# The query norm of the first layer's dense heads as one number per query, in the scale of the softmax's exponential

## The chip, the cores and the metric

The kernel runs on one core of a Trainium2 chip. The metric is the device time of one execution in microseconds (us). Five engines work side by side, each through its own queue in a fixed order: TensorE (PE; its loads of the stationary operand are shown as PEld), VectorE (DVE), ScalarE (ACT), GpSimd (POOL) and SyncE (SP), which here issues the large transfers. They meet by semaphores only.

## The reference

The program is an attention layer, a pooling layer and a second attention layer with a retention half, over 512 tokens of width 2048. The change touches the eight dense heads of the first layer. For these the reference computes, with 512 queries, 512 + 256 keys and a head size of 128:

```python
qA = _rope(_rmsnorm(qA, q_norm), cos, sin)
kA = _rope(_rmsnorm(kA, k_norm), cos, sin)
outA = _dense_attention(qA, jnp.concatenate([kA, kA_c], axis=1), jnp.concatenate([vA, vA_c], axis=1))

def _rmsnorm(x, g):
    y = xf * lax.rsqrt(jnp.mean(xf * xf, axis=-1, keepdims=True) + EPS)
    return (y * g.astype(jnp.float32)).astype(x.dtype)

# dense attention, per block of 128 queries
s = jnp.einsum('bqkgd,bskd->bkgqs', qb, k) * ATTN_SCALE
p = jax.nn.softmax(s, axis=-1)
```

The norm of a query is one number, so it can be left out of the rotation and of the product with the keys, and multiplied in afterwards: softmax(r s) needs exp(r s - max(r s)), and with r > 0 the maximum is r max(s).

## The kernel before

**Layout.** Queries and keys lie transposed: the 128 dimensions of a head on the partitions, the 512 tokens along the free axis. `QR[:, h % 2, :]` holds one head's queries, `KTA` the keys of four key heads, `VV` the values. The score of 128 queries against 768 keys lies in the PSUM tile `S` (queries on the partitions), of which there is one. The dense heads are 0 to 7; heads 8 to 15 are banded, without a norm. `TB` and `OB` are single PSUM banks for sums, transposes and the output of a head; `G` are four banks in two pairs, in which the projections are summed up.

**The stream that TensorE works through.** A projection unit makes 256 columns of `w_in` in four chunks of 512 rows. Each weight chunk is loaded to `RAW` by SP, rounded to `WHI` by ScalarE, its rest taken to `WLO` by VectorE (L1314), three buffers each; it is used in four steps of six matmuls (`G<-HHI,WHI`, `G<-HLO,WHI`, `G<-HHI,WLO` twice). A pair of heads, `p`, has two units: one for the gates z and one for the queries, so 32 steps in all. When the queries of pair p are done, `q_copy` takes the two banks to `QR`, and the task `pair_task(p)` then runs beside the 32 steps of the next pair: after each step one yield of the generator passes, and what it puts into the plan at that point stands there in the queue of every engine. The plan thus sets the order on all engines; nothing is moved at run time.

**pair_task before, dense pairs.** For each of the two heads in turn, `norm_rope` puts: the square (`nr_square`, ScalarE, `SQ2[1]`), two steps later the sum over the partitions (`nr_stat`: TensorE multiplies a matrix of ones with the squares, 128x512, into `TB`; ScalarE takes logarithm and exponential of all 128x512 into `TY`; VectorE makes `TM<-TB` and refines the root with three more instructions over 128x512), and a step later `nr_apply` (VectorE: query times gain times root into `TM`, L1320, then the rotation, four instructions at L1314). That is 8 steps, one more follows, and then the eight scores of the pair stand three steps apart: `score` (TensorE, `S<-KTA,QR`), `softmax` (VectorE: negated maximum of the row, L1501; ScalarE: `PB<-S,SM`, exp(S + nm), with the sum, L1132; VectorE: reciprocal L1510, product L1317), four or five steps later `turn` (transposes of `PB` into `TB` and `OB`, copied to `PT` by ScalarE), and seven steps after the fourth score of a head `pv` (`OB<-PT,VV`) and `gate`. Since there is one `S`, the matmuls of a score wait for the exponential of the score before (`a_exp`). In VectorE's queue the reciprocal stands right behind the maximum, so VectorE waits for each exponential.

**What else is in the same queues.** After every chunk one load of 512 KB for the modulation of later layers is multiplied up by VectorE (`mod_acc`, four instructions `MACC`, L1320); for every fourth of these `mod_sum` transposes the sums in `TB` (TensorE) and reduces them (VectorE, L1437). It is put in at a chunk's end or, if one is pending, right behind the next score. The gates' `silu_a` and `silu_b` follow behind the first unit of a pair.

## Time and profile before

| | |
|---|---|
| time, median of 3 runs | 2726.67 us (2721.63 to 2731.41) |
| profiled execution, its own time | 2726.54 us |
| its span | 2724.8 us |
| granted TensorE clock over the span | 0.975 of full |
| TensorE busy | 2596.8 us, 95% of the span |
| VectorE busy | 1728.5 us, 63% |
| ScalarE busy | 949.7 us, 35% |
| chain that ended last, by engine | PE 76%, DVE 14%, DMA 3%, ACT 3%, issue 3% |

The numbers come from one profiled execution. Busy time is a sum over stages that have different limits, so a stage is read by stretches. The dense heads of the first layer lie between 280 and 600 us of the span (the pairs start at about 280, 354, 432 and 508 us), the banded ones behind them up to 866 us. A wait is the idle time of an engine in front of an instruction, put down to what released it; the clock is a share of full speed, 2.4 GHz.

### The profile page before, as it was taken

The numbers are of one execution on the slowest core, as the hardware profiler recorded it, in microseconds if no ns is written. First come the engines' busy times: TensorE is split into PE (matmuls) and PEld (weight loads), VectorE is DVE, ScalarE is ACT, GpSimd is POOL, SyncE is SP. The second block draws the span as 40 slices with busy tenths as digits, with TensorE's granted clock in tenths as the row PEclk, the third lists the DMA queues.
The fourth block names the chain that finished last, engine by engine and source line by source line (L and its number), as shares of the span: only waits on it lengthen the run. The fifth ranks groups of instructions, "written<-read, shape, count | busy, mean of one in ns | idle before, by whom it ended". The sixth has DMA issues, their size and how long they took to land.

```text
span 2724.8 us, 31894 instructions
## 1 busy us (share of the span) xinstructions
PE 2596.8 (95%) x12675; PEld 2084.8 (77%) x12675; DVE 1728.5 (63%) x2880; ACT 949.7 (35%) x1510; POOL 134.2 (5%) x121
## 2 busy tenths in 40 slices
PE   7999999999988999999998998999999999999898
PEld 4789666677766887888776886877878878878686
DVE  4446777767775877777887877667465444445422
ACT  3232343343343333332323333344354422223221
POOL 0000000000000103000010112000000000000000
PEclk7999999999999998999999997999999999999999
DMA  9935433333334553656647553444222222322432
GB/s 349 328 134 161 132 99 105 118 113 124 122 107 147 197 185 128 205 169 205 190 155 244 188 182 134 141 142 147 70 78 86 82 82 89 98 83 82 150 117 70
DMA packets 358566, 390.71 MB, mean 143 GB/s; under 512 B 11842, under 2 KB 352450, under 8 KB 354578
## 3 DMA queue, kind: packets, MB, share of 16 engines
q1 hardware_dynamic: 352144, 354.79, 40.8%
q0 software_dynamic: 6128, 33.89, 3.3%
q8 instruction: 100, 1.64, 0.3%
q14 instruction: 48, 0.39, 0.0%
q10 hardware_dynamic: 146, 0.00, 0.0%
HBM read 371.85 MB, written 16.78 MB: 143 GB/s over the span
## 4 chain that ended last, share of the span: by engine, by line
PE 76%; DVE 14%; DMA 3%; ACT 3%; issue 3%; SPq 1%; POOL 0%; DVEq 0%; ACTq 0%; POOLq 0%
PE G L1765 63%; PE S L1765 5%; PE OB L1765 5%; DVE MACC L1320 4%; PE TB L1765 2%; DVE WLO L1314 2%; PE TB L1768 1%; DMA MRAW<-in_od_mod_w 1%; DMA MRAW<-in_w_ada 1%; DVE TT L1314 1%; ACT WHI L1006 1%; DMA MRAW<-in_ev_mod_w 1%; DVE Y L1314 1%; DVE SM L1501 1%; ACT PB L1132 1%
## 5 line engine op out<-in xcount | busy, mean ns | idle before, releaser
L1765 PE MATMUL G<-HHI,WHI 128*128 128x512 f32 x2624 | 1109.8, 423 | 41.0 <-issue 18.2
L1765 PE MATMUL G<-HHI,WLO 128*128 128x512 f32 x2624 | 1034.1, 394 | 0.0
L1765 PE MATMUL G<-HLO,WHI 128*128 128x512 f32 x2624 | 1031.6, 393 | 0.0
L1765 PEld LDWEIGHTS G<-HHI,WHI 128*128 128x128 f32 x2624 | 499.2, 190 | 165.5 <-issue 50.2
L1314 DVE TENSOR_TENSOR WLO<-RAW,WHI 128x1024 fp32r<-128x1024 f32 x376 | 458.2, 1221 | 259.8 <-ACT WHI L1006 257.0
L1006 ACT ACTIVATE WHI<-RAW 128x1024 fp32r<-128x1024 f32 x376 | 395.0, 1053 | 580.3 <-PE G L1765 539.7
L1765 PEld LDWEIGHTS G<-HLO,WHI 128*128 128x128 f32 x2624 | 499.4, 190 | 114.7 <-issue 19.2
L1765 PEld LDWEIGHTS G<-HHI,WLO 128*128 128x128 f32 x2624 | 497.2, 189 | 109.4
L1320 DVE SCALAR_TENSOR_TENSOR MACC<-MRAW,SC,MACC 128x256 f32<-128x256 f32 x840 | 431.8, 514 | 94.7 <-DMA MRAW<-in_od_mod_w 36.3
L1765 PE MATMUL G<-WHI,HHI 128*128 128x256 f32 x640 | 186.8, 292 | 0.0
L1765 PE MATMUL G<-WLO,HHI 128*128 128x256 f32 x640 | 181.5, 284 | 0.0
L1765 PE MATMUL G<-WHI,HLO 128*128 128x256 f32 x640 | 181.5, 284 | 0.0
L1132 ACT ACTIVATE PB<-S,SM 128x768 f32<-128x768 f32 (+2 forms) x64 | 52.6, 822 | 281.4 <-DVE SM L1317 161.1
L1765 PEld LDWEIGHTS G<-WHI,HHI 128*128 128x128 f32 x640 | 123.0, 192 | 8.0 <-issue 7.4
L1003 ACT ACTIVATE SQ<-SQ 128x512 f32<-128x512 f32 x144 | 90.8, 631 | 100.3 <-DVE SQ L1320 97.3
L1765 PEld LDWEIGHTS G<-WHI,HLO 128*128 128x128 f32 x640 | 123.1, 192 | 2.3 <-issue 1.7
L1765 PEld LDWEIGHTS G<-WLO,HHI 128*128 128x128 f32 x640 | 123.1, 192 | 0.0
L1765 PE MATMUL S<-KTA,QR 128*128 128x256 f32 (+2 forms) x256 | 86.0, 459 | 19.0 <-ACT PB L1132 19.0
L1765 PEld LDWEIGHTS S<-KTA,QR 128*128 128x128 f32 x256 | 47.3, 192 | 49.1 <-ACT PB L1132 24.6
L1765 PE MATMUL OB<-PT,VV 128*128 128x512 f32 (+2 forms) x192 | 77.0, 552 | 0.7 <-ACT PT L1006 0.7
L1317 DVE TENSOR_SCALAR TM<-TB 128x512 f32<-128x512 f32 (+1 forms) x36 | 24.3, 675 | 83.8 <-ACT TY L1003 83.8
L1003 ACT ACTIVATE TY<-TB,SM 128x512 f32<-128x512 f32 (+1 forms) x36 | 24.4, 678 | 141.0 <-PE TB L1765 141.0
(263 smaller groups left out, 2399.1 us busy)
## 6 DMA issues: line engine op xcount, KB each, us to landing
RAW<-in_w_in SPq DMA_DIRECT2D x128, 512.0 KB, 3.9
MRAW<-in_od_mod_w SPq DMA_DIRECT2D x96, 512.0 KB, 4.9
MRAW<-in_w_ada SPq DMA_DIRECT2D x96, 512.0 KB, 5.1
RAW<-in_ev_w_in SPq DMA_DIRECT2D x80, 512.0 KB, 3.9
RAW<-in_od_w_in SPq DMA_DIRECT2D x64, 512.0 KB, 4.1
MRAW<-in_ev_mod_w SPq DMA_DIRECT2D x54, 512.0 KB, 5.1
RAW<-in_ev_w_out SPq DMA_DIRECT2D x32, 512.0 KB, 3.5
RAW<-in_od_w_out SPq DMA_DIRECT2D x32, 512.0 KB, 3.5
```

Of the source, the lines that this page charges most:

```text
L1003: return e.o.activation(o, i, fn, bias=bias, scale=scale)
L1006: return e.o.activation(o, i, ACT.Copy, scale=scale)
L1132: e.o.activation(PB[n % 2][:, lo:768], S[:, lo:768], ACT.Exp, bias=nm, scale=1.0, accum_out=SM[:, i + 1:i + 2]).then_inc(*a_exp.up((h, qt)))
L1314: return e.o.tensor_tensor(o, a, b, op)
L1317: return e.o.tensor_scalar(o, a, s1, s2, op0, op1) if op1 else e.o.tensor_scalar(o, a, s1, None, op0)
L1320: return e.o.scalar_tensor_tensor(out=o, in0=a, scalar=s, in1=b, op0=op0, op1=op1)
L1501: e.o.tensor_reduce(nm, S[:, lo:768], AX_X, MAX, negate=True).then_inc(*v_sm.up((h, qt, "row"), (h, qt, "max")))
L1765: return e.o.matmul(o, l, r, start=start, stop=stop, skip_group_check=True)
L1768: return e.o.transpose(o, i, IDN[:, :])
```

## The change

The query copy of a dense head now multiplies by the gain (which already holds the factor 128^-0.5) on its way from `G` to `QR`, and ScalarE squares straight from `G` (into `SQ2[1]` and `TM`). The rotation runs on these, without the root. The sums of squares of both heads of a pair are made at once, as eight matmuls with the squares as the stationary operand and one column of ones as the moving one, so that they come out as a column of 128 queries each: `TB[:, 0:8]`. Mean, logarithm, exponential and refinement are made on 128x8. The root of a query then stands on the same partition as its score: the exponential takes it as its scale, and the negated maximum is multiplied by it in one more VectorE instruction. The generator yields five times ahead of the first score, where it did nine times.

```diff
+    QMEAN, QTEMP, QROOT = COL[:, 0:8], COL[:, 8:16], COL[:, 16:24]
+    QSQ = [SQ2[1], TM]
...
         def pair_task(p):
-            for i in range(2):
-                for _ in norm_rope(("q", 2 * p + i), p < 4):
-                    yield
+            yield
+            put("nr_apply", ("q", 2 * p))
+            yield
+            if p < 4:
+                put("q_stat", p)
+            yield
+            put("nr_apply", ("q", 2 * p + 1))
+            yield
+            if p < 4:
+                put("q_root", p)
             yield
...
+    def q_root_of(h, qt):
+        return QROOT[:, h % 2 * 4 + qt:h % 2 * 4 + qt + 1]
...
-                cp(QR[:, nt, :], G[pair][nt][:, :], SCALE if p >= 4 else 1.0).then_inc(*a_ev.up(("q", h)))
+                if p >= 4:
+                    cp(QR[:, nt, :], G[pair][nt][:, :], SCALE).then_inc(*a_ev.up(("q", h)))
+                else:
+                    e.wait_ge(v_intro, "q_scale")
+                    cp(QR[:, nt, :], G[pair][nt][:, :], COL[:, 152:153]).then_inc(*a_ev.up(("q", h)))
+                    e.wait_ge(*chain)
+                    if p:
+                        e.wait_ge(p_stat, ("q", p - 1))
+                    elif nt == 0:
+                        e.wait_ge(*sq[1])
+                    af(QSQ[nt][:, :], G[pair][nt][:, :], ACT.Square).then_inc(*a_sq.up(("q", h)))
+                    sq[1] = p_stat, ("q", p)
+            elif stage == "q_stat":
+                p, = a
+                e.wait_ge(v_rs, (("q", p), 1))
+                af(QROOT, QMEAN, ACT.Ln).then_inc(*a_rs.up((("q", p), 1)))
+                e.wait_ge(a_rs, (("q", p), 1))
+                af(QROOT, QROOT, ACT.Exp, 0.0, -0.5).then_inc(*a_rs.up((("q", p), 2)))
...
-                e.o.activation(PB[n % 2][:, lo:768], S[:, lo:768], ACT.Exp, bias=nm, scale=1.0,
+                e.o.activation(PB[n % 2][:, lo:768], S[:, lo:768], ACT.Exp, bias=nm,
+                               scale=1.0 if banded(h) else q_root_of(h, qt),
                                accum_out=SM[:, i + 1:i + 2]).then_inc(*a_exp.up((h, qt)))
...
-                if what == "kc" or what == "k" and h < 2 or what == "q" and h < 8:
+                if what == "kc" or what == "k" and h < 2:
...
+            elif stage == "q_stat":
+                p, = a
+                e.wait_ge(p_stat, ("q", p))
+                ts(QMEAN, TB[:, 0:8], 1.0 / 128, EPS, MUL, ADD).then_inc(*v_rs.up((("q", p), 1)))
+                sq[1] = p_stat, ("q", p)
+            elif stage == "q_root":
+                p, = a
+                e.wait_ge(a_rs, (("q", p), 2))
+                tt(QTEMP, QROOT, QROOT, MUL).then_inc(*v_rs.up((("q", p), 2)))
+                e.wait_ge(v_rs, (("q", p), 2))
+                stt(QTEMP, QTEMP, -0.5, QMEAN, MUL, MUL).then_inc(*v_rs.up((("q", p), 3)))
+                e.wait_ge(v_rs, (("q", p), 3))
+                stt(QROOT, QTEMP, 1.5, QROOT, ADD, MUL).then_inc(*v_rs.up((("q", p), 4)))
...
-                    *v_sm.up((h, qt, "row"), (h, qt, "max")))
-                if banded(h):
-                    e.wait_ge(v_sm, (h, qt, "row"))
+                    *v_sm.up((h, qt, "row")))
+                e.wait_ge(v_sm, (h, qt, "row"))
+                if not banded(h):
+                    e.wait_ge(v_rs, (("q", h // 2), 4))
+                    ts(nm, nm, q_root_of(h, qt), None, MUL).then_inc(*v_sm.up((h, qt, "max")))
+                else:
...
-                gf[pair][nt] = a_ev, ("q", 2 * p + nt)
+                gf[pair][nt] = (a_ev if p >= 4 else a_sq), ("q", 2 * p + nt)
+            elif stage == "q_stat":
+                p, = a
+                e.wait_ge(*tb)
+                for nt in range(2):
+                    e.wait_ge(a_sq, ("q", 2 * p + nt))
+                    for n in range(4):
+                        t = mm(TB[:, 4 * nt + n:4 * nt + n + 1], QSQ[nt][:, n * P:(n + 1) * P], ONE[:, 0:1], True, True)
+                t.then_inc(*p_stat.up(("q", p)))
+                tb = v_rs, (("q", p), 1)
```

The order on VectorE, from the second head of pair 0 to its first softmax. Before:

```order
L1317 TENSOR_SCALAR TM<-TB 128x512
L1314 TENSOR_TENSOR TT<-TY 128x512
L1320 SCALAR_TENSOR_TENSOR TT<-TT,TM 128x512
L1320 SCALAR_TENSOR_TENSOR TY<-TT,TY 128x512
L1320 SCALAR_TENSOR_TENSOR TM<-QR,COL,TY 128x512
L1314 TENSOR_TENSOR TT<-TM,SN 64x512 x2
L1314 TENSOR_TENSOR QR<-TM,CS 128x512
L1314 TENSOR_TENSOR QR<-QR,TT 128x512
L1314 TENSOR_TENSOR WLO_71<-RAW_65,WHI_68 128x1024
L1317 TENSOR_SCALAR MACC_76<-MRAW_74,SC 128x256
L1320 SCALAR_TENSOR_TENSOR MACC_76<-MRAW_74,SC,MACC_76 128x256 x3
L1501 TENSOR_REDUCE SM<-S 128x1
```

The same stretch after the change:

```order
L1347 TENSOR_SCALAR COL<-TB 128x8
L1344 TENSOR_TENSOR TT<-QR,SN 64x512 x2
L1344 TENSOR_TENSOR QR<-QR,CS 128x512
L1344 TENSOR_TENSOR QR<-QR,TT 128x512
L1344 TENSOR_TENSOR WLO_73<-RAW_67,WHI_70 128x1024
L1467 TENSOR_REDUCE MOD<-TB 128x2
L1344 TENSOR_TENSOR MOD<-MOD,COL 128x2
L1350 SCALAR_TENSOR_TENSOR MACC_77<-MRAW_75,SC,MACC_77 128x256 x4
L1344 TENSOR_TENSOR COL<-COL 128x8
L1350 SCALAR_TENSOR_TENSOR COL<-COL 128x8 x2
L1542 TENSOR_REDUCE SM<-S 128x1
L1347 TENSOR_SCALAR SM<-SM,COL 128x1
```

Five instructions over 128x512 are gone ahead of each rotation. `COL<-TB`, which waits for the column sums, now stands ahead of the second head's rotation, and the first softmax stands behind the weight rest of one chunk earlier (`WLO_73`), with the modulation's reduction between them.

The order on ScalarE from the query copies of pair 0 to its first exponential. Before:

```order
L1006 ACTIVATE QR<-G 128x512 x2
L1003 ACTIVATE SQ_79<-QR 128x512
L1003 ACTIVATE TY<-TB,SM 128x512
L1003 ACTIVATE TY<-TY 128x512
L1006 ACTIVATE WHI_70<-RAW_67 128x1024
...
L1006 ACTIVATE WHI_68<-RAW_65 128x1024
L1132 ACTIVATE PB_98,SM<-S,SM 128x768
```

After:

```order
L1018 ACTIVATE QR<-G,COL 128x512
L1015 ACTIVATE SQ_79<-G 128x512
L1018 ACTIVATE QR<-G,COL 128x512
L1015 ACTIVATE TM<-G 128x512
L1015 ACTIVATE COL<-COL 128x8 x2
L1018 ACTIVATE WHI_70<-RAW_67 128x1024
L1161 ACTIVATE PB_98,SM<-S,SM,COL 128x768
```

Both squares now stand right behind the copies, and one rounding of weights fewer lies ahead of the first exponential.

On TensorE the two sums over 128x512 of a pair become one block of eight one-column products, and the reduction of the modulation moves. After:

```order
L1809 MATMUL TB<-ONE,SQ_79 128x1 [waits s_a_sq,s_v_msum]
L1809 MATMUL TB<-ONE,SQ_79 128x1 x3
L1809 MATMUL TB<-ONE,TM 128x1 [waits s_a_sq]
L1809 MATMUL TB<-ONE,TM 128x1 x3
...
L1812 MATMUL TB<-IDN,MACC_76 128x128 [waits s_v_rs,s_v_acc]
```

The block stands after the third step behind the queries, as the first of the two sums did; the transposes of `MACC` follow a step later, and the first score after the sixth step instead of the tenth. In the first three pairs the last `pv` and `gate` of a pair now come at the second step of the next pair, ahead of the block, where they came at the sixth. The queues of POOL and SP are unchanged, and from the second score of the first banded pair on all queues are as before.

## Rows read from the trace of the kernel before

**Rows 1.** The page, part 1: busy us (share of the span) xinstructions.

```profile
PE 2596.8 (95%) x12675; PEld 2084.8 (77%) x12675; DVE 1728.5 (63%) x2880; ACT 949.7 (35%) x1510; POOL 134.2 (5%) x121
```

**Rows 2.** Waits of TensorE, 250 to 600 us: waited for: us, times, longest.

```profile
PE S L1765 <- ACT PB L1132: 8.2, 4, 2.1
PE TB L1765 <- DVE MOD L1437: 2.8, 1, 2.8
PE TB L1765 <- ACT PT L1006: 2.3, 3, 0.8
PE G L1765 <- DVE WLO L1314: 1.0, 3, 0.3
```

**Rows 3.** Timeline, pair 1: start, us, instruction xcount [idle before <-releaser].

```profile
384.86 1.67 PE L1765 MATMUL S<-KTA,QR 128*128 128x512 f32 x4 [2.06 <-ACT PB L1132]
```

**Rows 4.** Timeline of VectorE and ScalarE, second head of pair 0, first softmax.

```profile
300.55 1.40 DVE L1314 TENSOR_TENSOR TT<-TM,SN 64x512 f32<-64x512 f32 x2
...
303.32 1.22 DVE L1314 TENSOR_TENSOR WLO<-RAW,WHI 128x1024 fp32r<-128x1024 f32 x1
...
306.28 0.95 DVE L1501 TENSOR_REDUCE SM<-S 128x1 f32<-128x768 f32 x1
...
307.26 0.90 ACT L1132 ACTIVATE PB<-S,SM 128x768 f32<-128x768 f32 x1 [8.84 <-DVE SM L1501]
```

**Rows 5.** Stretches around the waits: length, busy per engine (x), granted clock, DMA.

```profile
291.00:299.00 8.00, 5.19 (x15) 3.38 (x14) 6.98 (x13) 2.27 (x3) 0.00 (x0) 0.79 0.40 132
...
384.00:393.00 9.00, 8.14 (x31) 6.31 (x32) 6.01 (x12) 3.35 (x6) 0.00 (x0) 0.81 0.52 175
...
462.00:471.00 9.00, 8.22 (x36) 5.95 (x37) 6.11 (x13) 3.36 (x7) 0.00 (x0) 1.00 0.54 178
...
538.00:548.00 10.00, 8.75 (x32) 6.39 (x33) 6.17 (x13) 3.92 (x7) 0.00 (x0) 0.83 0.52 176
```

**Rows 6.** Groups of instructions, 250 to 600 us: busy, mean ns | idle before.

```profile
L1317 DVE TENSOR_SCALAR TM<-TB 128x512 f32<-128x512 f32 x8 | 5.5, 691 | 17.3 <-ACT TY L1003 17.3
...
L1320 DVE SCALAR_TENSOR_TENSOR TM<-QR,COL,TY 128x512 f32<-128x512 f32 x8 | 6.0, 752 | 0.9
...
L1437 DVE TENSOR_REDUCE MOD<-TB 128x2 f32<-128x256 f32 x10 | 4.2, 421 | 2.7 <-PE TB L1768 2.7
...
L1006 ACT ACTIVATE QR<-G 128x512 f32<-128x512 f32 x10 | 5.5, 602 | 3.7 <-PE G L1765 3.7
```

**Rows 7.** The same over the whole span, one shape each.

```profile
L1006 ACT ACTIVATE Y<-G,MOD 128x512 f32<-128x512 f32 x32 | 22.0, 686 | 0.0
...
L1317 DVE TENSOR_SCALAR SM<-SM 128x1 f32<-128x1 f32 x32 | 6.9, 215 | 1.1
...
L1320 DVE SCALAR_TENSOR_TENSOR COL<-COL 128x4 f32<-128x4 f32 x8 | 1.3, 161 | 0.3
```

**Rows 8.** Chain that ended last, 250 to 620 us: start, us, what.

```profile
321.27 1.29 PE S L1765 x4
322.56 1.39 PE G L1765 x6
...
336.17 5.15 PE OB L1765 x12
...
449.63 0.87 PE TB L1765 x2
```

**Rows 9.** Timeline of TensorE at a block of one-column sums.

```profile
1015.43 1.93 PE L1765 MATMUL S<-ONE,SUM 128*128 128x1 f32 x16
1017.21 0.48 PE L1765 MATMUL G<-HHI,WHI 128*128 128x512 f32 x1
```

**Rows 10.** The stretch behind that block, columns as in Rows 5.

```profile
1018.00:1022.00 4.00, 4.00 (x16) 3.19 (x14) 0.00 (x0) 0.17 (x1) 0.00 (x0) 0.62 0.00 0
```

**Rows 11.** Timeline, pair 0 beside the gates: end of an exponential, next score.

```profile
332.60 0.19 ACT L1132 ACTIVATION_READ_ACCUMULATOR PB<-S,SM 128x1 f32 x1
...
333.32 1.45 PE L1765 MATMUL S<-KTA,QR 128*128 128x512 f32 x4
```

More of the change, by code:

```diff
@@ L1458, in dve_program @@
                     continue
-                if what == "kc" or what == "k" and h < 2 or what == "q" and h < 8:
+                if what == "kc" or what == "k" and h < 2:
                     e.wait_ge(v_rs, (key, 4))
-                    if what == "q":
-                        e.wait_ge(v_intro, "q_scale")
                     cur = TM[:, 0:n]
```

## The prediction

> **What bounds the kernel now.** I read the page first, then the waits of TensorE in the stretch of the dense heads, then the timelines around those waits, and last the granted clock there. The page has TensorE busy for 95% of the span [rows 1]: it works through one fixed queue, so the time is its work, its waits and what it loses at a lower clock. An edit on VectorE or ScalarE is worth only what it takes from these three. Between 250 and 600 us TensorE waits for 14.3 us in four sorts [rows 2]: four times for an exponential before a score can overwrite S (8.2), once for the modulation's reduction to free TB (2.8), three times for a copy out of TB (2.3) and three times for a weight rest (1.0). All lie at the starts of the four pairs. The wait for the exponential shows how it comes about [rows 3, 4]: the scores' own matmuls ran long before, but VectorE was still at the norm and rotation of the second head, then did a weight rest and the modulation, and reached the row maximum late; ScalarE had idled 8.84 us for it. The remaining 28 scores don't wait. The second thing at these places is the clock [rows 5]: it fell to 1.2 GHz for a part of three of the four stretches, behind waits of 2.8, 2.1 and 2.0 us, and stayed at 2.4 GHz in the fourth, behind a wait of the same length.
>
> **Part 1, VectorE's load.** Per dense head go four instructions of 0.69 us (the row of TM<-TB; the three of the refinement last the same) and one of 0.75 [rows 6]: 3.5 us, or 7.0 per pair. Added per pair are one mean and three steps of refinement on 128x8, priced at 0.16 by the 128x4 ones, together 0.6, and a product on 128x1 for each of eight scores at 0.22 [rows 7], 1.7. VectorE is relieved by 4.7 us a pair, 19 in all, none of which counts by itself.
>
> **Part 2, the start of a pair.** I lay the new order out by hand. T is the end of a pair's query unit; a step is 1.39, a score 1.29, a pv 5.15 [rows 8], the block of eight column sums 1.78 (sixteen records from 1015.43 to 1017.21, which is eight matmuls) [rows 9]. For pairs 1 to 3 TensorE has two steps, pv, a step and the block up to T+11.1, three steps and two short transposes up to T+15.7, the first score up to T+17.0 and, if nothing holds it, the second score from T+21.2. VectorE has finished the first rotation (2.8 us, from 300.55 to 303.32) [rows 4] at about T+7, the gate behind pv at T+8.8, and then stands still for the block: a new wait in line, with the second rotation, a weight rest and the modulation queued behind it. From T+11.3 it does the mean and that rotation (to T+14.2), weight rest and modulation (3.0 by 303.32 to 306.28) [rows 4], which with the reduction's 0.42 [rows 6] and its addition make 3.7 (to T+17.9), three root steps (0.5, to T+18.4), the maximum (0.95, to T+19.4) and its product (0.22); the exponential ends at about T+20.7. TensorE wants S at T+21.2. The wait of 2.06 is gone, by a margin of half a microsecond. The next score has less: maximum one comes behind another weight rest and modulation and its exponential ends about 0.4 after TensorE asks. Pair 0 has neither pv nor gate and comes out alike (a margin of 0.2, then 0.4 of wait). The wait for the weight rest goes too, since that rest is made six steps earlier than it is used. The waits on TB go, because the block comes after the last transposes of the old pair are copied and the modulation's transposes now stand behind it, a step after the mean has been read. I keep 1.3 us of waits out of 14.3: minus 13.0. The ends are minus 14.3 and, if each pair keeps its wait for the exponential and the weight rest, minus 5.1.
>
> **Part 3, TensorE's own work.** Eight sums at 0.87 [rows 8] go, 7.0; four blocks at 1.78 come, 7.1 [rows 9]. In TensorE's queue the three sums that waited for a copy and the one before the low clock cost more than 0.87, so the balance lies between 0 and minus 1; I take minus 0.5. Scores, transposes and pv are the same in number and only stand four steps earlier.
>
> **Part 4, the clock.** The three lowered stretches lost 8 x 0.21, 9 x 0.19 and 10 x 0.17, 1.7 each, 5.1 in all [rows 5]. With no wait near 2 us left they have no reason to come back. But a block of one-column sums is thin work of its own: behind a run of twelve of them with no wait the clock was at 0.62 for 4 us, a loss of 1.5 [rows 10]. The new block is two thirds as long. I take it that two of the four lower the clock, at 1.7 each: 3.4 against 5.1, minus 1.7. The ends are minus 5.1 (none) and plus 1.7 (all four).
> The Trainium skill (TensorE: Matmul & The Clock Gate, section "What's actually happening") puts the lower clock down to how busy TensorE has been, and its table of states names idle time alone as what brings it about. By that table the blocks would cost nothing, and this term would be minus 5.1 and the time 2708. The row above speaks against reading it so: there the engine was never idle.
>
> **Part 5, the scores beyond the first.** Each of the 32 exponentials starts later by the product (0.22) and lasts longer by its second pointer, priced by the copy with a column as its scale against the one without, 0.686 less 0.602 [rows 7, 6]: 0.08. So 0.3 us is added to the path from score to score, 32 times, 9.6 in all if nothing covered it. What covers it is the time until TensorE comes to the next score, three steps and transposes, 4.8 us, against 2.4 for the new path when VectorE is not behind. VectorE is most behind beside the gates' work: there an exponential ended 0.5 us before the score that needed it [rows 11]. In the new order the second gate falls beside a pv of 5.15 and not beside a score, so I count the cover as enough: 0, with 6 us (0.5 at three scores of each pair) as the other end. The query copies grow by 0.08 too; they have a whole unit until their banks are needed: nothing.
>
> **The sum.** -13.0 - 0.5 - 1.7 = -15.2 against the profiled execution's 2726.5 (span 2724.8 and 1.7 around it), which is also the runs' median of 2726.67: 2711.3.
>
> **Rivals.**
> A. Forecast, 2711, own range 2705 to 2717. Chance 0.55.
> B. The scores beside the gates wait. For it: the margin of 0.5 [rows 11] and 0.3 more on each path. Against it: the pv beside them, and 4.7 us less on VectorE per pair. It costs 6: 2717. Chance 0.16.
> C. All four blocks lower the clock. For it: rows 10; against it: the block is shorter, and clock and waits are lost together only in part. 2711.3 + 3.4 = 2715. Chance 0.13.
> D. The head of VectorE's line takes the gain away: it waits for the block ahead of the second rotation, and if what follows runs 2.3 us later than laid out (a late ScalarE for the logarithm, a late modulation load), each pair keeps its wait for exponential and weight rest, 9.2, and its low clock. That leaves -5.1 and -0.5: 2721. Against it: VectorE did the same tail of work in the time of the rows. Chance 0.10.
> E. Slower. Product and pointer lie open at every score: VectorE falls behind at the start of a pair and, with 0.3 more per score, never catches up, so TensorE waits at all 32 scores and at all starts as today. Then the waits stay and 32 x 0.3 is added, with nothing won but 0.5: 2736. It decides where VectorE is later than TensorE's arrival by the 0.5 us of rows 11 at every score; today that distance is kept at 28 of 32. Chance 0.04.
> F. More than forecast: no wait left and no lowered clock, -14.3 - 5.1 - 0.5: 2707. Chance 0.02 beyond the forecast's own range.
>
> **How the numbers follow.** The predicted time is A's, 2711.3. The range takes in the ends of waits and clock (2707) with some 3 us of the scatter of the three runs below it, and B and C together (2721) with 1 above: 2704 to 2722. It leaves out E and the far parts of D and F. A measurement of this kernel can tell about 0.3%, 8.2 us, from no change, so the border is 2718.5. A, F, most of C and over half of B are below it: 0.78 faster. D and the rest of B and C are within: 0.18. E: 0.04 slower.
>
> **What the changed profile would show.** Waits of TensorE from 250 to 600 us at 1 to 2 us, none of them above 0.6, if part 2 is right; 5 us or more with "S <- ACT PB" at the pairs' starts means D; small ones (0.1 to 0.6) at scores in the middle of a pair mean B, many of them E. VectorE shows an idle time of 2 to 3 us in front of COL<-TB in pairs 1 to 3, and the block lasts about 1.8. Granted clock of 1.00 around the blocks means minus 5.1 for the clock, 0.8 at each of them C. What would make the prediction wrong is above all a clock that falls elsewhere in later stages than before, which these rows can't tell, and a product on 128x1 that costs more than its 0.22 because it waits for the instruction ahead of it.

## The result, and the profile after

| | before | after |
|---|---|---|
| median of 4 runs | 2726.27 us | 2701.43 us (2697.87 to 2702.04) |
| ratio | 1 | 0.9906, 95% interval 0.9886 to 0.9926 |
| profiled execution, its own time | 2726.54 us | 2701.90 us |
| its span | 2724.8 us | 2700.1 us |
| first query copy of pair 0 to that of pair 4 | 311.09 us | 288.51 us |

The change makes the kernel 24.8 us faster. A second series of the changed kernel gave 2701.87 us (four runs, ratio 0.9907, 0.9892 to 0.9923). The forecast was 2711.3 with a range of 2704 to 2722: the sign was right, but the measured time lies below the range.

The last row of the table is the measure for all that follows. In the timeline of ScalarE it is the distance from the first `QR<-G` of the first dense pair to the first one of the first banded pair, so four whole pairs; I call it **the dense stretch**. Between two profiles of the same kernel it differs by 0.04 us (288.51 and 288.47), far less than the medians do. It holds 22.6 of the 24.8 us. TensorE's idle time in it is 14.5 us: the 14.3 of [rows 2] and one more wait of 0.2, for a mean on VectorE (`TB<-IDN,MACC`). Pair by pair, from one pair's query copy to the next:

| pair | before | after | less | idle of TensorE before | lowered clock before [rows 5] | rest |
|---|---|---|---|---|---|---|
| 0 | 78.77 | 71.17 | 7.60 | 5.01 | 8 x 0.21 = 1.68 | 0.91 |
| 1 | 77.86 | 72.44 | 5.42 | 3.18 | 9 x 0.19 = 1.71 | 0.53 |
| 2 | 76.53 | 72.46 | 4.07 | 3.17 | 0 | 0.90 |
| 3 | 77.93 | 72.44 | 5.49 | 3.16 | 10 x 0.17 = 1.70 | 0.63 |
| sum | 311.09 | 288.51 | 22.58 | 14.5 | 5.1 | 3.0 |

The rest is for the most part time that the idle time doesn't show. In the profile of before the second score of pairs 1 to 3 stands 8.27 us behind the first, in that of after 5.41. The two waits between them show 0.34 and 2.06 of idle time, 2.40 together; 0.46 more is lost. The wait of 0.78 ahead of the first sum makes a distance of 1.38 out of one that is 0.35 where nothing waits, so 0.25 more. With pair 0 read the same way (0.5) that is 2.7 us in all.

Part 1 of the page of the changed kernel (busy time, share, instructions):

```profile
PE 2587.7 (96%) x12723; PEld 2087.7 (77%) x12723; DVE 1711.4 (63%) x2888; ACT 943.3 (35%) x1502; POOL 133.1 (5%) x121
```

VectorE is relieved by 17.1 us against [rows 1], and TensorE is busy 9.1 us less. The waits of TensorE from 250 to 600 us, after (us in total, times, longest), to be held against the four rows of [rows 2]:

```profile
PE TB L1812 <- DVE MOD L1467: 0.6, 1, 0.6
```

That wait is at 595 us, behind the dense heads. In the dense stretch itself TensorE waits for nothing. The clock there, by stretches at the start of pair 1 (length; busy time of PE, PEld, DVE, ACT and POOL with their counts; granted clock; DMA share and GB/s):

```profile
353.00:355.00 2.00, 2.00 (x17) 1.87 (x15) 0.18 (x1) 0.00 (x0) 0.00 (x0) 1.00 0.00 0
355.00:357.00 2.00, 2.00 (x14) 1.71 (x13) 1.39 (x3) 1.22 (x3) 0.00 (x0) 1.00 0.00 0
```

The block of one-column sums runs from 353.67 to 355.4, and the clock stays at 2.4 GHz through it and behind it. It does so in the whole dense stretch, where [rows 5] had 0.79, 0.81 and 0.83 around the waits of pairs 0, 1 and 3. The timeline of TensorE there (start, us, instruction, count of records; without the products of the projection):

```profile
353.67 0.95 PE L1809 MATMUL TB<-ONE,SQ 128*128 128x1 f32 x8
354.48 1.03 PE L1809 MATMUL TB<-ONE,TM 128*128 128x1 f32 x8
...
359.80 1.45 PE L1809 MATMUL S<-KTA,QR 128*128 128x512 f32 x4
365.22 1.02 PE L1809 MATMUL S<-KTA,QR 128*128 128x512 f32 x2
```

and that of VectorE and ScalarE in the same microseconds:

```profile
355.55 0.17 DVE L1347 TENSOR_SCALAR COL<-TB 128x8 f32<-128x8 f32 x1 [2.37 <-PE TB L1809]
...
358.52 1.22 DVE L1344 TENSOR_TENSOR WLO<-RAW,WHI 128x1024 fp32r<-128x1024 f32 x1
...
360.19 2.04 DVE L1350 SCALAR_TENSOR_TENSOR MACC<-MRAW,SC,MACC 128x256 f32<-128x256 f32 x4
...
362.63 0.95 DVE L1542 TENSOR_REDUCE SM<-S 128x1 f32<-128x768 f32 x1
363.62 0.21 DVE L1347 TENSOR_SCALAR SM<-SM,COL 128x1 f32<-128x1 f32 x1
```

```profile
363.87 0.99 ACT L1161 ACTIVATE PB<-S,SM,COL 128x768 f32<-128x768 f32 x1 [6.72 <-DVE SM L1347]
364.76 0.19 ACT L1161 ACTIVATION_READ_ACCUMULATOR PB<-S,SM,COL 128x1 f32 x1
```

This is the schedule that part 2 laid out by hand, rotation, weight rest, modulation, root, maximum, product. The exponential's last record ends at 364.95 and the next score writes `S` at 365.22: in place of the wait of 2.06 [rows 3] there is a margin of 0.27 us. VectorE stands still for 2.37 us in front of `COL<-TB`, and nobody waits for that.

The groups of the new instructions, 250 to 600 us (busy, mean ns of one | idle before):

```profile
L1161 ACT ACTIVATE PB<-S,SM,COL 128x768 f32<-128x768 f32 x32 | 31.8, 993 | 120.4 <-DVE SM L1347 120.4
L1347 DVE TENSOR_SCALAR SM<-SM,COL 128x1 f32<-128x1 f32 x32 | 6.9, 215 | 1.1
L1018 ACT ACTIVATE QR<-G,COL 128x512 f32<-128x512 f32 x8 | 5.5, 690 | 3.1 <-PE G L1809 3.1
L1350 DVE SCALAR_TENSOR_TENSOR COL<-COL 128x8 f32<-128x8 f32 x8 | 1.3, 167 | 0.3
```

All four prices were as taken: the product 0.22 (215), the exponential 0.09 longer than the 0.90 of [rows 4] (0.08 was taken), the query copy 690 against the 602 of [rows 6], the refinement 167 against the 161 of [rows 7].

### The profile page after: what moved, and what is told of

Same layout as the page of the kernel before. It is cut to its first block, busy times and chain, and to the rows that moved or that the text cites. A ratio compares the mean times of both kernels' runs of the same rounds, so it can differ in the third digit from the quotient of the medians.

```text
span 2700.1 us, 31982 instructions
## 1 busy us (share of the span) xinstructions
PE 2587.7 (96%) x12723; PEld 2087.7 (77%) x12723; DVE 1711.4 (63%) x2888; ACT 943.3 (35%) x1502; POOL 133.1 (5%) x121
## 4 chain that ended last, share of the span: by engine, by line
PE 79%; DVE 12%; DMA 3%; ACT 3%; issue 2%; SPq 1%; POOL 0%; DVEq 0%; ACTq 0%; POOLq 0%
PE G L1809 65%; PE S L1809 5%; PE OB L1809 5%; DVE MACC L1350 4%; PE TB L1809 2%; DVE WLO L1344 2%; PE TB L1812 1%; DMA MRAW<-in_w_ada 1%; ACT WHI L1018 1%; DMA MRAW<-in_ev_mod_w 1%; DVE Y L1344 1%; DVE HLO L1344 1%; DVE TT L1344 1%; DMA MRAW<-in_od_mod_w 1%; ACT PB L1161 1%
## 5 line engine op out<-in xcount | busy, mean ns | idle before, releaser
L1161 ACT ACTIVATE PB<-S,SM 128x512 f32<-128x512 f32 (+1 forms) x32 | 23.8, 742 | 163.9 <-DVE SM L1347 163.9
L1161 ACT ACTIVATE PB<-S,SM,COL 128x768 f32<-128x768 f32 x32 | 31.8, 993 | 120.4 <-DVE SM L1347 120.4
L1344 DVE TENSOR_TENSOR WB<-S,DK 128x512 f32<-128x512 f32 (+3 forms) x32 | 15.7, 491 | 83.2 <-PE S L1809 83.2
```

Source lines behind the costliest of these rows:

```text
L1161: e.o.activation(PB[n % 2][:, lo:768], S[:, lo:768], ACT.Exp, bias=nm, scale=1.0 if banded(h) else q_root_of(h, qt), accum_out=SM[:, i + 1 ...
L1344: return e.o.tensor_tensor(o, a, b, op)
```

## The experiments

The change does three things at once: it takes work off VectorE, it puts the start of a pair four steps earlier, and it makes TensorE's sums another way and both at once, so that the second head's rotation no longer stands behind a sum of its own. Theory 1 was that VectorE's load ahead of the first maximum decides, theory 2 that the earlier place does. For the clock the question was why four blocks of thin products did it no harm. The kernels start from the changed one unless said otherwise. Times of one run are marked so; the dense stretch is given for each.

### The nine yields back

```diff
                 put("q_root", p)
+                for _ in range(4):
+                    yield
```

> The changed kernel with four more yields ahead of the first score, so that the scores stand where they stood in the kernel before; the numbers and instructions are those of the change. Theory 1 (VectorE's shorter work ahead of the first softmax gave the gain): no wait for an exponential comes back, since VectorE now has 5.5 us more. The block of column sums falls behind the last transposes of the old pair again and waits for their copy, some 0.8 us in three pairs: dense stretch 289 to 292, clock 1.00, time 2702 to 2706. Theory 2 (the earlier place of the scores gave it, by clearing pv and gate from the start of a pair): half or more of the 22.6 us comes back, dense stretch 300 or more, time above 2712.

Measured: 2711.35 us (ratio 0.9942, 0.9925 to 0.9960), dense stretch 298.88. So 10.4 of the 22.6 us come back, between the two theories. The waits of TensorE in it:

```profile
PE TB L1811 <- ACT PT L1020: 2.1, 3, 0.7
PE S L1811 <- ACT PB L1163: 1.5, 4, 0.4
```

They are 3.6 us. The waits for the first exponentials' late maximum are gone even at the old place: the second score follows the first by 5.41, as in the changed kernel. The four waits for an exponential stand beside the gates, at the sixth score of a pair. Those of the block for the copy of the old pair's transposes are back, as in [rows 2]. The other part is the clock, at the block of pair 1:

```profile
353.00:355.00 2.00, 2.00 (x10) 1.56 (x10) 1.90 (x5) 0.30 (x2) 0.00 (x0) 0.81 0.68 239
355.00:357.00 2.00, 2.00 (x7) 1.68 (x6) 1.90 (x4) 1.42 (x4) 0.00 (x0) 0.50 0.00 0
357.00:359.00 2.00, 2.00 (x8) 1.57 (x8) 2.00 (x3) 0.97 (x2) 0.00 (x0) 0.83 0.00 0
```

Here the block stands behind short transposes and a wait of 0.70, and the clock falls to 1.2 GHz behind it; it costs 2 x 0.19 + 2 x 0.50 + 2 x 0.17 = 1.7 us. It does so in pairs 1 to 3, 5.1 us; with the 3.6 and some 0.2 more for each of the seven waits that is 10.1 of the 10.4. In the changed kernel the same block stands between projection steps and lowers nothing. So the changed work at the old places takes 12.2 us off the kernel before, and the new places another 10.4.

### VectorE's load put back at the new places

One, three or ten products over 128x512 are added to a pair's rotations, their result unused: one or three ahead of the second head's, or five ahead of each head's.

```diff
+                    if what == "q" and h < 8 and h % 2 in (1,):
+                        for x in range(3):
...
+                            tt(TT_[:, 0:n], CS[:, 0:n], SN[:, 0:n], MUL).then_inc(*v_nr.up((key, "load", x)))
```

> The changed kernel with one more product over 128x512 (0.7 us) on VectorE ahead of the second head's rotation. The traces of the change show the first exponential 0.3 us and the second 0.1 us ahead of the score that needs S. Theory 1: the first second-score wait opens at 0.3 to 0.5 us and the next at 0.1 to 0.3, in each of four pairs: 2 to 3 us of waits for an exponential, no lower clock, dense stretch 290.5 to 292. If the margin is wider than it looks: 288.5.

> As the run with one more product ahead of the second head's rotation, with three (2.1 us). One product opened a wait in each pair whose idle time shows as 0.2 us while the pair grew by 0.61: a wait costs about 0.4 more than its idle time, since the ends of matmuls are modelled. So here the first exponential comes 1.8 us behind the score that needs it: idle time 1.6 to 1.8 in each of four pairs, 6.4 to 7.2 in all, dense stretch 288.5 + 4 x 2.0 = 296.5. If the clock falls behind such waits (it did at 2.0 in the kernel before, three times of four), up to 1.5 more for each: up to 302.

> The changed kernel with five more products over 128x512 on VectorE ahead of the rotation of each dense head, 3.5 us a head, written to scratch: the old load at the new places. Theory 1: the first head's load is partly hidden in VectorE's wait for the block (2.4 to 3.0 us of it), the second's is not; VectorE comes 4 to 4.6 us later to the first softmax, TensorE waits 3.5 to 4.5 us in each pair, and the clock falls behind such waits: dense stretch 304 to 312, time 2717 to 2725. Theory 2 (place of the scores alone): dense stretch below 292, time below 2705.

Measured:

| added per pair | dense stretch | more per pair | time |
|---|---|---|---|
| nothing | 288.51 | | 2701.43 |
| 1 product (0.7 us) | 290.94 | 0.61 | 2704.44 (one run) |
| 3 products (2.2 us) | 296.74 | 2.06 | 2710.48 (one run) |
| 10 products (7.2 us) | 310.22 | 5.4 (3.96 to 6.41) | 2722.61, ratio 0.9989 (0.9979 to 0.9998) |

In the kernel with ten, TensorE's idle time is again a wait for the first exponential of each pair (and one trifle):

```profile
PE S L1815 <- ACT PB L1161: 14.2, 4, 3.5
```

and in pair 1:

```profile
377.25 1.56 PE L1815 MATMUL S<-KTA,QR 128*128 128x512 f32 x4 [3.54 <-ACT PB L1161]
```

From the first 0.1 to 0.3 us on, what is added to VectorE in front of the second rotation is paid by TensorE one for one. Of the ten, half stand ahead of the first head's rotation, where VectorE stood still before (2.4 us in front of `COL<-TB`, 0.5 in front of the gate): in pair 3 the first maximum comes 4.0 us later, not 7.2. The second score of each pair then stands 9.18 behind the first, 3.77 more than the 5.41 of the changed kernel. That is nearly all that pair 3 grew by, 3.96, and its clock stayed at 2.4 GHz. Pairs 0 to 2 grew by 5.93, 5.41 and 6.41, since behind the same wait their clock fell, here in pair 1:

```profile
378.00:380.00 2.00, 2.00 (x7) 1.44 (x6) 1.63 (x3) 0.14 (x1) 0.00 (x0) 0.67 0.04 14
380.00:382.00 2.00, 2.00 (x6) 1.53 (x5) 1.93 (x4) 0.00 (x0) 0.00 (x0) 0.50 0.66 190
```

So of the 21.7 us some 15.5 are waits, with what their idle time doesn't show, and some 6 are the clock, as in the kernel before. With VectorE as late as that the new places hold next to nothing of the gain (0.9 us). The load isn't quite that of before: the mean, the root's refinement and the product with it, 0.9 us ahead of the first exponential, are still there too.

### VectorE relieved at the old places

The kernel before, with the three products over 128x512 that refine the queries' root left out; that refinement is missing from the computation.

```diff
             ts(TM[:, 0:n], bank, 1.0 / count, EPS, MUL, ADD).then_inc(...)
             e.wait_ge(a_rs, (key, 2))
+            if key[0] == "q":
+                return
```

> The kernel before, without the three products over 128x512 that refine each query root on VectorE (the refinement is left out; everything else and the order stay). VectorE is relieved of 6 x 0.69 = 4.1 us a pair, nearly what the change relieves (4.7). Theory 1 (VectorE's load ahead of the first row maximum decides): the waits for the exponential and the weight rest, 9.2 of 14.5 us, go, those on TB (5.1) stay, some of the lowered clock goes; the dense stretch (first query copy of pair 0 to that of pair 4) shrinks from 311.1 to between 297 and 302. Theory 2 (the new places alone bring the gain): it stays at 308 or more.

Measured: 2712.21 us (ratio 0.9948, 0.9933 to 0.9963), dense stretch 297.48. 4.1 us less on VectorE per pair, with nothing moved, bring 13.6 of the 22.6 us. Only half of the 4.1 counts, though. Pair 1, before and then without the refinement:

```profile
373.39 0.69 DVE L1317 TENSOR_SCALAR TM<-TB 128x512 f32<-128x512 f32 x1 [1.50 <-ACT TY L1003]
...
382.83 0.95 DVE L1501 TENSOR_REDUCE SM<-S 128x1 f32<-128x768 f32 x1
```

```profile
365.63 0.69 DVE L1317 TENSOR_SCALAR TM<-TB 128x512 f32<-128x512 f32 x1 [2.27 <-ACT TY L1003]
...
372.98 0.95 DVE L1503 TENSOR_REDUCE SM<-S 128x1 f32<-128x768 f32 x1
```

The query copies are at 356.25 and 348.50. `TM<-TB` of the second head starts 17.1 us behind them in both: it stands behind TensorE's second sum and ScalarE's logarithm, and the three products taken from the first head only lengthen VectorE's idle time, by 1.2 in front of the gate and 0.8 in front of `TM<-TB`. The first maximum comes 2.1 earlier, by the three of the second head. So what made it late in the kernel before was this chain, sum, logarithm, mean, refinement, rotation, weight rest, modulation, and not VectorE's load as such. The change takes the sum and ScalarE's part out of its end too; no run does that alone. The waits left:

```profile
PE S L1767 <- ACT PB L1132: 2.5, 4, 0.7
PE TB L1767 <- ACT PT L1006: 2.3, 3, 0.8
PE TB L1767 <- DVE MOD L1439: 1.1, 1, 1.1
PE TB L1770 <- DVE TM L1317: 0.2, 1, 0.2
```

Of the waits of [rows 2], those for the exponential fell from 8.2 to 2.5, the weight rest's are gone, those for the copy out of `TB` stayed at 2.3. That is 8.4 us less idle time. The granted clock from 250 to 600 us is 1.00 here, with 0.99 before: the 5.1 us of lowered clock went with the waits near 2 us, as part 4 had it. The two make 13.5.

### The block of one-column sums twice and three times

The matmuls are repeated, which leaves their result as it was.

```diff
-                    for n in range(4):
+                    for n in [0, 1, 2, 3] * 2:
```

> The changed kernel with each block of column sums made twice into the same columns (16 matmuls, 3.6 us), to see whether thin work lowers the clock. In the changed kernel eight of them between full matmuls left it at 1.00; with the scores four steps later, where 0.7 us of waiting and transposes stand directly ahead of the block, it fell in three pairs (0.83 over 10 us, 1.7 us each). If thin work alone lowers it: dense stretch 288.5 + 4 x 1.7 for the work, 295.4, and 1.5 to 1.8 more for each block behind which it falls, up to 302, clock below 1.00 behind the blocks. If it takes an idle time: 295.4 and the clock stays at 1.00. In both the mean comes 1.8 us later to VectorE, which the later first score covers.

> The same with each block made three times (24 matmuls, 5.3 us). If thin work alone lowers the clock it surely does here: work 288.5 + 4 x 3.4 = 302.1, and 2 us or more for each fall, 308 or more. If it takes an idle time: 302.

Measured: 305.04 and 318.74 for the dense stretch, 2713.63 and 2731.11 us (one run each). The first is outside what either theory gave, by 3 us. The added eight matmuls are 1.7 us a pair, 6.8; the stretch grew by 16.5. The rest is the clock, at pair 1 of the doubled block:

```profile
359.32 1.84 PE L1809 MATMUL TB<-ONE,SQ 128*128 128x1 f32 x16
361.02 1.93 PE L1809 MATMUL TB<-ONE,TM 128*128 128x1 f32 x16
```

```profile
361.00:363.00 2.00, 2.00 (x19) 2.00 (x19) 0.01 (x1) 0.00 (x0) 0.00 (x0) 1.00 0.00 0
363.00:365.00 2.00, 2.00 (x6) 1.56 (x6) 1.90 (x4) 1.37 (x3) 0.00 (x0) 0.54 0.04 8
365.00:367.00 2.00, 2.00 (x7) 1.52 (x7) 1.97 (x3) 0.00 (x0) 0.00 (x0) 0.61 0.00 0
```

TensorE is busy in every one of these microseconds, and the clock falls to 1.2 GHz just behind the block. It loses 2 x 0.46 + 2 x 0.39 = 1.7 us; with the 1.7 of the added matmuls that is 3.4, and the pair grew by 3.34. At pair 0 the low stretch is twice as long:

```profile
284.00:286.00 2.00, 2.00 (x14) 2.00 (x13) 0.00 (x0) 0.00 (x0) 0.00 (x0) 0.66 0.00 0
286.00:288.00 2.00, 2.00 (x7) 1.61 (x7) 1.64 (x4) 1.37 (x3) 0.00 (x0) 0.50 0.00 0
288.00:290.00 2.00, 2.00 (x7) 1.58 (x6) 1.97 (x3) 0.00 (x0) 0.00 (x0) 0.50 0.00 0
290.00:292.00 2.00, 2.00 (x7) 1.54 (x6) 1.89 (x6) 0.00 (x0) 0.00 (x0) 0.63 0.11 23
```

The block runs there from 281.91, so the clock fell before it had ended. 3.4 us are lost, and that pair grew by 4.97. Pairs 0 and 2 pay 3.4, pairs 1 and 3 pay 1.7. With the block made three times the pairs grow by 8.4, 6.8, 8.3 and 6.7, of which 3.4 is the work: 5.0 or 3.4 is lost. So rival C's mechanism is real, at the price of the forecast or twice that, but eight matmuls of a column between projection steps don't bring it about. Where it begins is known only between bounds: at none of 32 such blocks in the changed kernel and its variants whose blocks stand so (eight profiles), behind a run of twelve in the kernel before [rows 10], and at all four of sixteen. The Trainium skill (TensorE: Matmul & The Clock Gate, "What's actually happening") names in its table of states only idle time as what brings the 1.2 GHz level about. The doubled block speaks against reading it so: no idle, and the level was there at each of the four blocks.

### The path from score to score

Three kernels: one without the norm of the dense queries in the softmax (neither root as the exponential's scale nor product; the queries' norm is missing from the computation), one with two more products on 128x1 ahead of the root's, and one with the mean and root stages put behind the second rotation, so that VectorE doesn't stand in front of them.

```diff
-                    ts(nm, nm, q_root_of(h, qt), None, MUL).then_inc(*v_sm.up((h, qt, "max")))
...
-                               scale=1.0 if banded(h) else q_root_of(h, qt),
+                               scale=1.0,
```

> The changed kernel without the product on the negated maximum and without the root as the exponential's scale: it leaves the norm of the dense queries out of the softmax. The path from score to score is 0.3 us shorter at each of 32 scores. If it is covered, as the traces show (no wait in the dense stretch): 288.5 again, time near 2701. If hidden waits shorter than what the trace shows lie at the scores: up to 9 us less.

```diff
+                    for x in range(2):
+                        ts(nm, nm, ONE[:, 0:1], None, MUL).then_inc(*v_sm.up((h, qt, "one", x)))
+                        e.wait_ge(v_sm, (h, qt, "one", x))
                     ts(nm, nm, q_root_of(h, qt), None, MUL).then_inc(*v_sm.up((h, qt, "max")))
```

> The changed kernel with two more products of VectorE on 128x1 ahead of the product with the root, in each of the 32 dense softmaxes: 0.42 us more from score to score. Theory 1 (the path is covered by the time until TensorE's next score, with margins of 0.3 and 0.1 us at the first two exponentials of a pair only): waits of 0.1 to 0.8 at the second and third score of each pair, about 3 us in all, the dense stretch goes from 288.5 to between 290 and 293. Rival (the path lies open at many scores, beside the gates above all): waits at more than half of the 32 scores, the stretch 297 or more.

```diff
             put("nr_apply", ("q", 2 * p + 1))
+            if p < 4:
+                put("q_mean", p)
```

> The changed kernel with the mean, logarithm and exponential put behind the second head's rotation, so that VectorE doesn't stand still in front of them. The block of one-column sums stays where it is. Theory 1 (the head-of-line wait of 2.4 to 3 us costs nothing now, since no wait of TensorE hangs on it): VectorE's idle time ahead of the mean is gone or below 0.5, the first maximum comes up to 2 us earlier, the dense stretch stays at 288.5 within 0.3. Rival (the head-of-line wait still takes something away): the stretch becomes shorter by over 0.5.

Measured, dense stretch: without the norm 288.29, with two more products 298.75, with the mean later 288.29 (one run each: 2702.75, 2709.36, 2702.07). Product and pointer cost nothing now (0.2 us), and so does VectorE's stand in front of the mean (with the mean later that idle time is 0 and the first maximum comes 0.9 earlier). But the cover is thin. 0.42 us more on each path cost 2.6 us a pair. Idle time shows at two scores, one of them where neither I nor the forecast's main line had looked:

```profile
442.61 1.56 PE L1812 MATMUL S<-KTA,QR 128*128 128x512 f32 x4
...
449.37 1.56 PE L1812 MATMUL S<-KTA,QR 128*128 128x512 f32 x4 [0.42 <-ACT PB L1161]
...
461.89 1.45 PE L1812 MATMUL S<-KTA,QR 128*128 128x512 f32 x4
469.27 1.56 PE L1812 MATMUL S<-KTA,QR 128*128 128x512 f32 x4 [1.11 <-ACT PB L1161]
```

The one at 469.27 stands beside the gates, rival B's place. The changed kernel there, in pair 1 (end of the exponential, next score):

```profile
389.42 0.19 ACT L1161 ACTIVATION_READ_ACCUMULATOR PB<-S,SM,COL 128x1 f32 x1
...
389.90 1.45 PE L1809 MATMUL S<-KTA,QR 128*128 128x512 f32 x4
```

A margin of 0.29 us, where [rows 11] had 0.5. My expectation of 290 to 293 was wrong by 6 us: it counted the first scores' margins and forgot this one, and it took the 0.42 once. The 0.42 adds up instead, since VectorE has hardly a pause between a pair's scores that isn't a wait for the score or the exponential itself. Measured from the query copy, the first exponential of a pair ends 0.5 us later than in the changed kernel, the next ones 1.0, 1.5 and 2.0, and the fifth 2.5. In pair 1, with the query copy at 347.90, the fifth ends at 394.20:

```profile
394.01 0.19 ACT L1161 ACTIVATION_READ_ACCUMULATOR PB<-S,SM,COL 128x1 f32 x1
```

TensorE had lost 1.0 by then and the margin was 0.29, so 1.2 of the 2.5 is left as a wait.

The rows of pair 2 also show what idle time leaves out. In the changed kernel the same scores of pair 2 stand so:

```profile
437.65 1.45 PE L1809 MATMUL S<-KTA,QR 128*128 128x512 f32 x4
443.74 1.53 PE L1809 MATMUL S<-KTA,QR 128*128 128x512 f32 x4
...
456.27 1.45 PE L1809 MATMUL S<-KTA,QR 128*128 128x512 f32 x4
462.37 1.45 PE L1809 MATMUL S<-KTA,QR 128*128 128x512 f32 x4
```

From 437.65 to 443.74 are 6.09 us. With the two products the score before 449.37 is at 442.61, so 6.76: 0.67 more for an idle time of 0.42. At the other place it is 7.38 against 6.10: 1.28 for 1.11. At two further scores of the pair 0.3 us is lost each, with no idle time shown. The three added products of the load kernel gave 1.85 (7.26 against 5.41) for 1.69. So a wait of TensorE costs some 0.2 us more than the idle time in front of it. The ends of its matmuls are modelled in these profiles and can run into the wait; that this is the reason isn't shown.

### The banded pairs

The dense stretch has no wait left; the banded heads behind it still have waits for the exponential. As an attempt at a faster kernel, the second head's rotation was put one step earlier in the four banded pairs.

```diff
+            else:
+                put("nr_apply", ("q", 2 * p + 1))
             yield
-            put("nr_apply", ("q", 2 * p + 1))
+            if p < 4:
+                put("nr_apply", ("q", 2 * p + 1))
```

> The changed kernel, and in the four banded pairs the second head's rotation one step (1.39 us) earlier; the dense pairs are as in the change. If the waits of TensorE behind the dense heads (8.0 us in eight times for an exponential between 563 and 880 us, longest 2.2) come from VectorE reaching the first maximum late, as they did in the dense pairs before, they fall by about 1.4 us at each pair's first wait, to between 2 and 5 us, and the time from 2701.4 to between 2696 and 2699. If something else sets them (the weight rest or the modulation, which stand in line at fixed places), they stay at 8 and the time at 2701.

Measured: 2700.55 us (2696.55 to 2703.80, ratio 0.9900, 0.9883 to 0.9916), not to be told from the change, and it can't be: between the old and the new place of the rotation nothing else enters a queue, so that the built program has the same instructions in the same order, with the same waits, on every engine. The edit tests nothing of what was expected of it. The run is a third series of the changed kernel, and its differences are scatter: 8.6 us of waits for an exponential from 563 to 880 us in nine times, against 8.0 in eight.

One of them shows what a banded pair's first wait hangs on. In pair 5, first in the profile of the change, then in this one, VectorE and TensorE:

```profile
634.07 2.05 DVE L1350 SCALAR_TENSOR_TENSOR MACC<-MRAW,SC,MACC 128x256 f32<-128x256 f32 x4 [2.69 <-DMA MRAW<-in_od_mod_w]
648.17 2.22 PE L1809 MATMUL S<-KTA,QR 128*128 128x384 f32 x4 [2.20 <-ACT PB L1161]
```

```profile
633.84 2.05 DVE L1353 SCALAR_TENSOR_TENSOR MACC<-MRAW,SC,MACC 128x256 f32<-128x256 f32 x4 [2.08 <-DMA MRAW<-in_od_mod_w]
647.94 1.34 PE L1812 MATMUL S<-KTA,QR 128*128 128x384 f32 x4 [1.58 <-ACT PB L1164]
```

VectorE stands still for a load of the modulation and then works without a pause up to the maximum. The load came 0.6 us earlier in the second profile, and TensorE's wait is 0.6 shorter. So here the late arrival of a load counts like work; how long VectorE waits for it changes from profile to profile, and no run moved it.

## Where the prediction was right, and where it failed

The time came out 9.9 us below the forecast and 2.6 below its range. The mechanism was right; two terms of the sum failed by their size, the waits (part 2) and the clock (part 4):

| term | forecast | measured |
|---|---|---|
| part 2, waits | -13.0 | -14.5 of idle time and -2.7 that it doesn't show: -17.2 |
| part 3, own work | -0.5 | what is left of the dense stretch: -0.3 |
| part 4, clock | -1.7 | -5.1 |
| part 5, path | 0 | 0 |
| outside the dense stretch | none | -2.2, open |
| sum | -15.2 | -24.8 |

**What bounds the kernel.** Right. TensorE's waits and its clock at the starts of the four pairs were the whole of it, and the experiments on VectorE's load show that its lateness made the largest of them.

**Part 1 and the prices.** Right within 0.02 us each. The relief is 19 in all by the forecast and 17.1 by the page. What part 1 left out, though [rows 6] have it, is VectorE's idle time of 17.3 us in front of `TM<-TB`: the refinement of the first head stood ahead of such a wait and counted for nothing, as the run without it shows, and the wait itself was part of what made the first maximum late.

**Part 2, the waits (-13.0), failed by 4.2.** The mechanism was right, the size not. The layout gave the first exponential a margin of 0.5 (0.27 measured) and the second one a lateness of 0.4 (a margin of 0.1 measured: its last record ends at 371.22, the next score starts at 371.32). It had TensorE and VectorE both some 1.7 us later than they came, since one projection step stands ahead of pv, not two: with T at 345.9 the exponential laid out to end at T+20.7 ended at T+19.0, and the score laid out for T+21.2 came at T+19.3. The 1.3 us of waits that were kept didn't appear (one more, of 0.2, wasn't in the count). And the term took waits at their idle time: the twelve of them cost 2.7 us more.

**Part 3, TensorE's own work (-0.5).** Right in kind. A block is 1.7 long, four are 6.8 against the 7.0 of the eight sums. The table's rest, 3.0, leaves 0.3 for this term once the hidden parts of the waits are taken off; that is as exact as the reading of those parts.

**Part 4, the clock (-1.7), failed by 3.4.** It let two of four blocks lower the clock; none did, so the term is its own lower end, -5.1. [rows 10] stood behind a run of twelve thin products (the eight of [rows 9] and four ahead of them), and a block of eight was taken as two thirds of the way to the same effect. The runs don't bear that out: eight between projection steps cost nothing at any pair, sixteen cost 1.7 or 3.4 at every pair, and eight behind transposes and a wait of 0.70 cost 1.7 at three pairs. Why eight don't and twelve did stays open.

**Part 5, the path (0).** Right: 0.2 us without product and scale. It rested on less than the text had it, 0.1 us at the second score and 0.29 beside the gates, and not on 4.8 against 2.4.

**The rivals.** None of B to E came. B was 0.3 us away, by the run with two more products. C was one block length away. D's wait in VectorE's line was there (2.37 us) and took nothing away, by the run with the mean later. E would have needed VectorE late at every score. Its mechanism is there, a lateness that grows from score to score and isn't caught up within the pair, but it takes more than the change adds: with 0.42 us more on each path waits showed at two of eight. F, no wait and no lowered clock, is what happened, and had been given 0.02: it was built from the same ends, but as if both together were unlikely, and its 2707 lay within the forecast's own 2705 to 2717. They hang together: where the waits near 2 us went, the clock stayed up, as the relieved kernel at the old places shows. Even F is 5 us short of the measured time: 2.7 us of hidden waits and the 2.2 outside the stretch.

**The sum again.** The dense stretch holds 22.6; the medians differ by 24.8. In the profile of before the first query copy is at 277.48, in that of after at 274.63, and every engine's instructions ahead of it are the same in the two kernels. The relieved kernel of before had it at 274.35, the load kernel with ten products at 276.97. That is scatter of the first part; behind the dense stretch the changed kernel's profile is 0.7 us the longer one. All this is of the size of the 2.2, and 22.6 lies within the interval of the ratio (20.2 to 31.1 us). Whether any of it belongs to the change stays open.

## What to carry to other kernels

Before a wait is costed, follow the late engine's queue back to its last pause. What is taken away behind that pause pays one for one down to the next margin (three products of the second head: 2.1 us). What is taken away ahead of it only makes the pause longer (three of the first head: nothing). Take a wait of TensorE as its idle time and some 0.2 us, and count the lowered clock that stands behind a wait together with the wait: the two went together here. Before more is added to a path that seems covered, list the margin at every place of the period, and add up what each step adds where the engine has no pause in between: here 0.42 us at each of eight scores was 2.5 at the fifth, and cost 2.6 us a pair. And before an order is tried on the chip, see that the queues have changed at all.

## What the runs showed of the hardware

- Sixteen matmuls with one column each (3.6 us) bring TensorE from 2.4 to 1.2 GHz without any idle time, at four of four places. Eight (1.7 us) don't where full matmuls stand before and behind them (32 places in eight profiles), and do behind short transposes and a wait of 0.70 us (three of three). A wait of 0.78 us in front of two sums over 512 columns didn't lower it (three places before the change, three in the relieved kernel). The low level lasted until 1.7 us were lost in some pairs and 3.4 in others, in one and the same kernel.
- In the dense stretch it fell behind a wait of 3.5 us in front of a score at three of four places, behind one of 2.0 to 2.1 at two of four, behind one of 1.7 at none of four.
- A wait of TensorE is longer than the profile's idle time: by 0.25, 0.17 and 0.16 us at three waits, and 0.31 us were lost at a score for which no idle time is shown at all (5.72 against 5.41 us between two scores).
- A column as the scale of an activation costs 0.09 us: 690 against 602 ns over 128x512, and, with a column as its bias too, 993 against 902 ns over 128x768.
